# The second lookup list's product and additions on GpSimd, in the routing of a two-layer diffusion backbone

## The reference, cut to what matters

```python
q = (h @ w_q).reshape(t, P_HEADS, 2, P_KEY_DIM // 2)
s = jnp.einsum('thpd,hpnd->thpn', q, sub_keys)          # two lists of 128 scores
sv, si = lax.top_k(s, P_TOPK)                           # 16 best of each list
cand = sv[:, :, 0, :, None] + sv[:, :, 1, None, :]
best, ci = lax.top_k(cand.reshape(t, P_HEADS, 256), P_TOPK)
i1 = jnp.take_along_axis(si[:, :, 0], ci // P_TOPK, axis=-1)
i2 = jnp.take_along_axis(si[:, :, 1], ci % P_TOPK, axis=-1)
experts = i1 * P_N_KEYS + i2
gates = jax.nn.softmax(best, axis=-1)
```

## Time and profile before

| | us |
|---|---|
| median of 3 runs | 4532.8 (4532.34 to 4536.46) |
| the profiled execution | 4533.72 |
| its span | 4531.9 |
| TensorE busy | 4031.5 (89%) |
| VectorE busy | 3620.1 (80%) |
| ScalarE busy | 1835.0 (40%) |
| GpSimd busy | 1117.4 (25%) |

### The profile page before, as it was taken

The page is one execution under the profiler, slowest core; times in us unless marked ns, Lnnn a source line. Parts: engine busy times, 40 slices in busy tenths (PEclk is TensorE's granted clock), DMA queues, the critical chain, the costliest instruction groups (busy, mean ns, idle before and its releaser), DMA issues. The chain is left out here.

```text
span 4531.9 us, 67116 instructions
## 1 busy us (share of the span) xinstructions
PE 4031.5 (89%) x22357; PEld 3485.8 (77%) x22357; DVE 3620.1 (80%) x7073; ACT 1835.0 (40%) x3314; POOL 1117.4 (25%) x1094
## 2 busy tenths in 40 slices
PE   7977978999889999999999977898936899999998
PEld 6964437899778888888888856644735899999998
DVE  4295783897979999999999954644799799999998
ACT  3224642101744444444444333354305544444443
POOL 0000000002943433444343300000007433232332
PEclk9957998965999999999999978699978999999998
DMA  4101221134689999999999911001204899999997
GB/s 176 52 1 35 66 79 56 52 112 149 188 322 379 375 375 372 378 377 371 382 376 370 371 48 47 18 1 37 64 30 125 315 370 370 375 372 373 370 372 283
DMA packets 246329, 1017.98 MB, mean 225 GB/s; under 512 B 16976, under 2 KB 115376, under 8 KB 145984
## 3 DMA queue, kind: packets, MB, share of 16 engines
q0 software_dynamic: 85824, 602.70, 34.3%
q1 hardware_dynamic: 160320, 413.17, 25.5%
HBM read 963.31 MB, written 52.43 MB: 224 GB/s over the span
## 5 line engine op out<-in xcount | busy, mean ns | idle before, releaser
L484 PE MATMUL psA<-h_hi,split_hi 128*128 128x448 f32 (+3 forms) x2768 | 974.5, 352 | 128.1 <-DVE xT L2324 55.3
L1208 POOL DMA_INDIRECT rows<-rows,pick_i x512 | 795.2, 1553 | 1156.3 <-DVE y_tok L2345 644.2
L1757 DVE TENSOR_TENSOR split_lo<-raw,split_hi 128x1024 fp32r<-128x1024 f32 x596 | 727.5, 1221 | 353.9 <-ACT split_hi L1249 352.0
L484 PE MATMUL psA<-h_lo,split_hi 128*128 128x448 f32 (+3 forms) x2768 | 952.2, 344 | 0.0
L484 PE MATMUL psA<-h_hi,split_lo 128*128 128x448 f32 (+3 forms) x2768 | 952.0, 344 | 0.0
L1249 ACT ACTIVATE split_hi<-raw 128x1024 fp32r<-128x1024 f32 x596 | 628.2, 1054 | 326.9 <-DMA raw<-expert_pairs 153.0
L484 PEld LDWEIGHTS psA<-h_hi,split_hi 128*128 128x128 f32 x2768 | 526.9, 190 | 215.2 <-issue 142.2
L2333 DVE CUSTOM_DVE_ANT_1 rows<-rows,h_wide 128x1024 f32<-128x1024 f32 x512 | 624.2, 1219 | 10.4 <-DMA rows<-rows,pick_i 8.2
L2345 DVE SCALAR_TENSOR_TENSOR y_tok<-rows,pick_w,y_tok 128x1024 f32<-128x1024 f32 x444 | 568.8, 1281 | 5.9
L484 PEld LDWEIGHTS psA<-h_hi,split_lo 128*128 128x128 f32 x2768 | 527.3, 190 | 36.0
L484 PEld LDWEIGHTS psA<-h_lo,split_hi 128*128 128x128 f32 x2768 | 528.5, 191 | 32.2
(11 more groups left out here) (304 smaller groups left out, 6606.2 us busy)
## 6 DMA issues: line engine op xcount, KB each, us to landing
raw<-expert_pairs SPq DMA_DIRECT2D x256, 1024.0 KB, 7.2
gates<-g_buf SPq DMA_DIRECT2D x24, 2048.0 KB, 8.7
raw<-tiles SPq DMA_DIRECT2D x84, 512.0 KB, 3.5
raw<-mod_tiles SPq DMA_DIRECT2D x80, 512.0 KB, 3.5
g_in<-gates POOLq DMA_DIRECT2D x32, 896.0 KB, 8.9
g_in<-gates POOLq DMA_DIRECT2D x32, 640.0 KB, 5.8
mod_w<-mod_pairs SPq DMA_DIRECT2D x8, 1024.0 KB, 18.0
rows<-rows,pick_i POOLq DMA_INDIRECT x512, 8.5
```

Source lines behind the costliest of these rows:

```text
L484: ins = nc.tensor.matmul(out_, lhsT, rhs, start=start, stop=stop)
L1208: nc.gpsimd.indirect_dma_start(rows[l][:, b, :], None, (rows0, rows1)[l], bass.IndirectOffsetOnAxis(pick_i[:, u:u + 1], 0))\
L1757: V.tensor_tensor(split_lo[:, n % SPLIT].rearrange("p k n -> p (k n)"), raw[:, n % RAW, :], split_hi[:, n % SPLIT].rearrange("p k n -> p ( ...
```

## The change

VectorE makes both comparisons at the start, the second list's into a buffer of its own (`eq2`), and raises `eq_second` after it. It then does product and additions of the first list as before. GpSimd waits for `eq_second`, does the product and the four additions of the second list in `eq2` and `eq2_sum`, each waiting for the one before, and raises `sel_second` at the last one. VectorE waits for `sel_second` after the reciprocal.

```diff
--- before.py
+++ after.py
@@ -246,6 +246,9 @@
     cand_raw = semaphore("cand_raw")
     cand_exp = semaphore("cand_exp")
     sel_ready = semaphore("sel_ready")
+    eq_second = semaphore("eq_second")
+    sel_second = semaphore("sel_second")
+    pool_tree = semaphore("pool_tree")
     sel_copied = semaphore("sel_copied")
     oh_ready = semaphore("oh_ready")
     oh_first = semaphore("oh_first")
@@ -381,6 +384,8 @@
     eq = in_r("eq", 44032, [P, P, TOPK], BF16)
     eq_sum = in_r("eq_sum", 48128, [P, P, TOPK], BF16)
     cand2 = in_r("cand2", 0, [P, PH, NCAND])
+    eq2 = in_r("eq2", 3072, [P, P, TOPK], BF16)
+    eq2_sum = in_r("eq2_sum", 8192, [P, P, TOPK], BF16)
     code = in_r("code", 38400, [P, 4, PH * TOPK], U32)
     best = in_r("best", 53248, [P, PH, TOPK])
     best_i = in_r("best_i", 53760, [P, PH, TOPK], U32)
@@ -1162,6 +1167,22 @@
             pool.wait_ge(mix_ready, seen.upto(mix_ready, KD))
             pool.dma_start(keysT[:], keys[l]).then_inc(keys_landed, 16)
 
+            def then_add(o_, a, b, sem=pool_tree):
+
+                nc.gpsimd.tensor_tensor(o_, a, b, ALU.add).then_inc(sem, 1)
+                pool.wait_ge(sem, seen.upto(sem))
+
+            for tt in route_order(l):
+                pool.wait_ge(eq_second, seen.upto(eq_second))
+                sit = si_b[:, tt].rearrange("p (h two) a -> p h two a", two=2)
+                e4 = eq2[:].rearrange("p (h k) a -> p h k a", h=PH)
+                nc.gpsimd.tensor_tensor(e4, e4, sit[:, :, 1, :].unsqueeze(2).broadcast_to([P, PH, TOPK, TOPK]), ALU.mult).then_inc(pool_tree, 1)
+                pool.wait_ge(pool_tree, seen.upto(pool_tree))
+                then_add(eq2_sum[:, :, 0:8], eq2[:, :, 0:8], eq2[:, :, 8:16])
+                then_add(eq2_sum[:, :, 8:12], eq2_sum[:, :, 0:4], eq2_sum[:, :, 4:8])
+                then_add(eq2_sum[:, :, 12:14], eq2_sum[:, :, 8:10], eq2_sum[:, :, 10:12])
+                then_add(sel[:, 1], eq2_sum[:, :, 12], eq2_sum[:, :, 13], sel_second)
+
             tb0, tb1 = gate_blocks(l)
             pool.wait_ge(sel_copied, seen.upto(sel_copied, NTT - DENSE[l][0] // P))
             base = 3 + l * (DENSE[0][1] // TB) * GROUPS
@@ -2228,26 +2249,27 @@
                 dve.wait_ge(dve_chain, seen.upto(dve_chain))
                 V.tensor_tensor(best[:], best[:], small[:, 128:136].unsqueeze(2).broadcast_to([P, PH, TOPK]), ALU.subtract).then_inc(cand_raw, 1)
                 dve.wait_ge(cand_raw, seen.upto(cand_raw))
-                for two in range(2):
-                    V.tensor_tensor(eq[:], ab_f[:, two].unsqueeze(2).broadcast_to([P, P, TOPK]),
-                                             iota16.unsqueeze(1).broadcast_to([P, P, TOPK]), ALU.is_equal).then_inc(dve_chain, 1)
-                    dve.wait_ge(dve_chain, seen.upto(dve_chain))
-                    e4 = eq[:].rearrange("p (h k) a -> p h k a", h=PH)
-                    V.tensor_tensor(e4, e4, sit[:, :, two, :].unsqueeze(2).broadcast_to([P, PH, TOPK, TOPK]), ALU.mult).then_inc(dve_chain, 1)
-                    dve.wait_ge(dve_chain, seen.upto(dve_chain))
-                    V.tensor_tensor(eq_sum[:, :, 0:8], eq[:, :, 0:8], eq[:, :, 8:16], ALU.add).then_inc(dve_chain, 1)
-                    dve.wait_ge(dve_chain, seen.upto(dve_chain))
-                    V.tensor_tensor(eq_sum[:, :, 8:12], eq_sum[:, :, 0:4], eq_sum[:, :, 4:8], ALU.add).then_inc(dve_chain, 1)
-                    dve.wait_ge(dve_chain, seen.upto(dve_chain))
-                    V.tensor_tensor(eq_sum[:, :, 12:14], eq_sum[:, :, 8:10], eq_sum[:, :, 10:12], ALU.add).then_inc(dve_chain, 1)
-                    dve.wait_ge(dve_chain, seen.upto(dve_chain))
-                    V.tensor_tensor(sel[:, two], eq_sum[:, :, 12], eq_sum[:, :, 13], ALU.add).then_inc(dve_chain, 1)
-                    dve.wait_ge(dve_chain, seen.upto(dve_chain))
+                for two in (1, 0):
+                    V.tensor_tensor((eq, eq2)[two][:], ab_f[:, two].unsqueeze(2).broadcast_to([P, P, TOPK]),
+                                    iota16.unsqueeze(1).broadcast_to([P, P, TOPK]), ALU.is_equal).then_inc((dve_chain, eq_second)[two], 1)
+                dve.wait_ge(dve_chain, seen.upto(dve_chain))
+                e4 = eq[:].rearrange("p (h k) a -> p h k a", h=PH)
+                V.tensor_tensor(e4, e4, sit[:, :, 0, :].unsqueeze(2).broadcast_to([P, PH, TOPK, TOPK]), ALU.mult).then_inc(dve_chain, 1)
+                dve.wait_ge(dve_chain, seen.upto(dve_chain))
+                V.tensor_tensor(eq_sum[:, :, 0:8], eq[:, :, 0:8], eq[:, :, 8:16], ALU.add).then_inc(dve_chain, 1)
+                dve.wait_ge(dve_chain, seen.upto(dve_chain))
+                V.tensor_tensor(eq_sum[:, :, 8:12], eq_sum[:, :, 0:4], eq_sum[:, :, 4:8], ALU.add).then_inc(dve_chain, 1)
+                dve.wait_ge(dve_chain, seen.upto(dve_chain))
+                V.tensor_tensor(eq_sum[:, :, 12:14], eq_sum[:, :, 8:10], eq_sum[:, :, 10:12], ALU.add).then_inc(dve_chain, 1)
+                dve.wait_ge(dve_chain, seen.upto(dve_chain))
+                V.tensor_tensor(sel[:, 0], eq_sum[:, :, 12], eq_sum[:, :, 13], ALU.add).then_inc(dve_chain, 1)
+                dve.wait_ge(dve_chain, seen.upto(dve_chain))
                 dve.wait_ge(cand_exp, seen.upto(cand_exp))
                 V.tensor_reduce(small[:, 136:144], best[:], AX.X, ALU.add).then_inc(dve_chain, 1)
                 dve.wait_ge(dve_chain, seen.upto(dve_chain))
                 V.reciprocal(small[:, 136:144], small[:, 136:144]).then_inc(dve_chain, 1)
                 dve.wait_ge(dve_chain, seen.upto(dve_chain))
+                dve.wait_ge(sel_second, seen.upto(sel_second))
                 starts = [t0 // P for t0, _ in GATHERED[l]]
                 if tt in starts:
                     j = starts.index(tt)
```

## The result

The changed kernel takes 4549.6 us in the median of 6 runs (4546.63 to 4553.88), against 4532.57 (4528.3 to 4536.46) for the kernel before on the same chip: 17.0 us between the medians. The ratio (of the means) is 1.0039, with a 95% interval of 1.0026 to 1.0052, or 11.8 to 23.6 us. Slower, as forecast, but by 17 us where 45.6 had been forecast.

A forecast was written before the change was run, and what follows sets the result against it. VectorE was taken to bound layer 1's routing, TensorE layer 0's. Layer 1's 25.2 us and layer 0's 20.4 made +45.6: 4533.7 + 45.6 - 0.9 = 4578.4 us, range 4534 to 4618.

The forecast's parts named there:

- 17.4 us over six tiles: Layer 0 routing, bound by TensorE: delay of VectorE's last sel that costs no time, 1088.28 against 1105.70.
- x: Time added per routing tile, from VectorE's first comparison to the product writing sel; forecast +6.3 us.
- its formula: Layer 0 routing's cost: six tiles' added time less the free 17.4 us; forecast 20.4 us.
- Rival A: Routing: engines don't block each other, GpSimd takes 10.4 us, +0.9 us per tile; 4536.5 us in all, chance 15%.
- B: Routing: GpSimd hides wholly behind VectorE, under 6.2 us, each tile losing 3.3 us; 4519.6 us in all, chance 12%.
- C: Routing: GpSimd at 3.3 ns per element plus blocking, 20.6 us, +11.1 us per tile; 4626 us in all, chance 15%.
- GpSimd alone: Second list's product and four additions on GpSimd, unblocked, with gaps and hand-overs: 10.4 us per tile, bounds 5.5 to 15.2.
- the forecast's 4 to 9: Main case for the time added per routing tile, 4 to 9 us: 4555 to 4605 us in all, chance 58%.
- GpSimd's chain: GpSimd's second-list work per routing tile, including standing still while VectorE reads two inputs: 10.4 + 5.4 = 15.8 us.
- the segment: Routing tile from VectorE's first comparison to the product writing sel: 18.1 us in place of 11.8.
- The blocking: GpSimd stands still during VectorE's two-input comparison, product and four additions in each routing tile: 5.4 us.
- the last sentence of the prediction: If VectorE's first-list instructions in routing are stretched instead, the blocking goes the other way, with the same sum.

The follow-up runs named there:

- e1_alone: Changed kernel, but VectorE waits for GpSimd's whole tree before starting the first list's comparison; 4572.9 us, ratio 1.0091 to the kernel before the change.
- e2_quarters: Changed kernel with GpSimd's product cut into four instructions of 512 elements; 4550.9 us, ratio 1.0042 to the kernel before the change.
- e6_swapped: Changed kernel with the first list's comparison before the second's, so GpSimd starts after both; 4549.5 us, ratio 1.0038 to the kernel before the change.
- e4_after_sums: Changed kernel, but GpSimd's tree runs beside the next tile's search, candidate sums made first, each layer's last tile on VectorE; 4523.8 us against 4532.7 before.

## Why the prediction was wrong

**What held.** The sign; that layer 1 pays each microsecond of a tile four times and layer 0 only beyond 17.4 us over six tiles (at x = 3.23 its formula gives 2.0 and the trace 2.1; at x = 5.4 both 15.0); that the engines exclude each other and little hides (2.2 us per tile, by e1_alone); that the rest of the program only starts later. Rival A (no blocking) and B (all hidden) fell with e1_alone and e2_quarters, C (15.2 us for GpSimd alone) with the 8.71 us of e1_alone. The wide range, 4534 to 4618, holds the measured time, but by luck: no case that the prediction names has x = 3.2, which lies between A's 0.9 and the forecast's 4 to 9.

**What failed** is the size of one term, "GpSimd's chain becomes 10.4 + 5.4 = 15.8 us", and with it the segment of 18.1 us, which is 15.0. Three parts:

- GpSimd alone: 10.4 predicted, 8.7 measured. The elements and fixed parts came to 4.04 + 2.12 + 1.73 + 0.41 = 8.3 us where 9.2 was put: 1.9 ns per element (the 1.92 us between 1024 and 2048 elements) where the middle of two far bounds had given 2.1. The gaps between them are 0.08 us each, where 0.25 had been taken from a single pair of copies.
- The blocking: 5.4 us predicted, but GpSimd's five instructions are stretched by only 1.92 + 0.86 + 0.33 + 0.06 + 0.04 = 3.2 us against their lengths alone. Part of each exchange passes beside the other engine's work: VectorE's product of 1.22 us holds GpSimd's addition for 0.86, the addition of 0.69 holds the next for 0.33. Two of VectorE's additions cost GpSimd next to nothing.
- The other way, 0.8 us were missing: VectorE's own list is now stretched to the end of GpSimd's chain (its last addition ends 0.24 us after), so sum and reciprocal come behind it, where the prediction had them finished.

Together -1.7 - 2.2 + 0.8 = -3.1 us per tile, 18.1 to 15.0. The step from there to 30 us of error is the multiplier: 4 in layer 1 and, beyond the slack, 6 in layer 0, 10 x 3.1 = 31. Layer 1 was put at 25.2 us and cost 12.9, layer 0 at 20.4 and cost 2.1: its first 2.9 us per tile are free, and the true 3.2 lies just above them. An estimate of x near such a threshold should be given on both sides of it; the range from 4 to 9 us lay wholly above. So the signs came out smaller too: the transposes of layer 1 are 26.86 us apart, not about 30, and in layer 0 TensorE idles once, 2.0 us before the last ones, where 7, then 2 to 3, and 9 us had been foretold.

**The direction of the blocking** was also wrong. From the gate stage, where VectorE's two-input instructions never stretch, the prediction took it that VectorE always wins. With GpSimd's long instructions VectorE stands, so of the signs foretold the idle of 9 to 10 us before L2268 and the unstretched first list did not come; the last sentence of the prediction had named this case. Why VectorE is never held in the gate stage stays open. That GpSimd's instructions are short there (0.2 to 0.7 us) doesn't explain it, for VectorE's comparison at 1199.77 starts inside one of GpSimd's (1199.30 to 1200.01, as far as its rough spans tell) and takes its usual 0.55 us all the same:

```profile
1199.30 0.71 POOL L1184 TENSOR_SCALAR onehot<-cst,first_key 128x128 f32<-128x128 f32 x1
```

The Trainium skill ("SBUF — State Buffer", section "Who interferes with whom", on the shared port pair) says that the first to start holds the pair, and that with two SBUF inputs VectorE contends with a GpSimd instruction that reads. By that rule the traces of the routing agree, with 4.95 us for 1.22 in the changed kernel, 1.22 again where VectorE starts first (e6_swapped), and MAX8 unstretched in e4_after_sums; the gate stage's 0.55 us is not what it would give. The direction changed the sum by the 0.8 us above, inside the 1 us foreseen.

The Trainium skill's price for an addition of 2048 fp32 elements ("GPSIMD Engine Reference", section "Performance versus the Vector engine"), 4497 ns, lies above this bf16 product of the same length, which takes 4.04 us alone.

## What to carry to other kernels

Moving two-input work from VectorE to GpSimd beside other two-input work bought nothing here: but for 2.2 us of 17.2 per tile the times add, and GpSimd's is 2.6 times as long (8.7 us for 3.3). Move it beside work that doesn't stretch, which here were the searches, put even the shortest two-input instruction ahead of the hand-over, and look for the wait in stretched instructions, as it isn't shown as idle time. Before sizing such a term, multiply its uncertainty by the number of times that the path takes it.

## What the runs showed that was not expected

- A VectorE instruction of 0.39 us takes 2.19 when it meets a GpSimd addition of 1024 elements: the wait is set by the other's length.
- A one-input TENSOR_SCALAR of VectorE goes from 0.23 to 0.37 us when it meets GpSimd's addition of 256 elements (e4_after_sums), while MAX8 and FIND_INDEX8 run past additions and products in their usual steps.
- Four short GpSimd products of 512 elements take 8.00 us beside VectorE, one of 2048 takes 5.96: pieces let the other engine in at each boundary, and move the wait from VectorE to GpSimd without changing the sum (15.1 against 15.0 us).
- GpSimd's tensor_tensor costs 4.04, 2.12, 1.04, 0.61 and 0.42 us for 2048, 1024, 512, 256 and 128 bf16 elements: 1.92 us more for the second 1024, so some 0.2 us are fixed.
